# Sparse-attention scores of a decoder layer: native f32 products replaced by three f32r products of high and low parts

## The chip, the cores and the metric

The kernel runs on one core of one Trainium2 chip. The metric is the device time of one execution in microseconds (us). Beside the timed runs there is one profiled execution, and every duration quoted from the trace is of that one.

## What is computed

One decoder layer on 512 tokens of width 1024, in float32: RMSNorm, one combined input projection, two attentions (a sparse one with 8 heads of 64, a dilated one with 12), a gated merge, an output projection, a SwiGLU feed-forward, and a final RMSNorm. The change touches the scores of the sparse attention, for its selected blocks and its window. In the reference, shortened:

```python
def block(i):                                   # 128 queries
    qb = queries * 64 ** -0.5; kb, kwb = keys of the selected blocks, keys of the window
    top, idx = lax.top_k(score, n_top)          # n_top = min(16, 8 blocks): all blocks
    ss = jnp.einsum('bqghd,bgqnld->bghqnl', qb, ks)
    ps, _ = masked_softmax(ss - m * ds, mask_s)   # causal, ALiBi
    o_s = jnp.einsum('bghqk,bgqkd->bqghd', ps, vs)
    sw = jnp.einsum('bqghd,bkgd->bghqk', qb, kwb)
    pw, _ = masked_softmax(sw - m * dw, mask_w)   # the window of 512 covers the sequence
    o_w = jnp.einsum('bghqk,bkgd->bqghd', pw, vwb)
    o = gate_c * o_c + gate_s * o_s + gate_w * o_w
```

With 512 tokens all blocks are selected and the window reaches over the whole sequence, so both branches are full causal attentions with their own keys (two branches b = 0, 1) and the same queries.

## The kernel before

Nearly all dense products are made as three f32r matmuls of high and low parts: `split_product` (L1427 to L1429) adds hi·hi, hi·lo and lo·hi in one PSUM bank. The parts of the weights are made per unit of 256 columns: `split_hi` on ScalarE (L585) casts the raw unit to f32r, `split_lo` on VectorE (L862) subtracts it from the raw values. The small attention products stay native f32.

Every engine walks one list, `SCHEDULE`, and does its own part of each job in that order. From about 223.8 us to 351 us the list interleaves the sparse attention with the projection tiles of the merge gates (units 15 to 21). A tile there is cut in two "parts" of 12 matmuls each. After its second part come "evac" (`gate_of_merge`: VectorE L998 takes it out of PSUM, ScalarE L659 applies tanh) and, for the first tile of a unit, "next_unit" (`split_hi` and `split_lo` of the unit after).

The sparse attention has 20 steps. Step n serves pair j = n // 5 of heads (one in each group, on partitions 0 to 63 and 64 to 127) and the segments of n % 5: (b, i) is branch b, query tile i, whose causal row has 128(i + 1) keys. Each step fills 512 columns of two banks:

```python
NSA_STEPS = [((0, 3),), ((0, 0), (0, 2)), ((0, 1), (1, 1)), ((1, 3),), ((1, 0), (1, 2))]
```

`scores` (L1629) makes them on TensorE, one 64-row matmul per head and segment; the two heads use different halves of the array rows. `reduce` (VectorE, L1176) adds the bias and takes the maximum, `exps` (ScalarE, L676) the exponentials, `scale` (VectorE: L1186, L1197, L1202) the sum's inverse and the gate, `turn` transposes on TensorE (L1642) with a copy by ScalarE (L740), `out` multiplies by v (L1661; for the first step of a pair L1656 too). One round of the list holds two steps: scores n and n + 1; turn n - 2; reduce, exps n; a part; scale n; turn n - 1; reduce, exps n + 1; the second part, its evac and perhaps next_unit; scale n + 1; out. So there are 10 bursts of scores, each of two steps. (In the rounds of n % 5 = 1 out n - 2 comes before turn n - 1.)

In the rounds of n = 8 and n = 12 the end of the list, the same for all engines, is in the code

```python
        parts(1)                                  # tile 44 (46): part, evac, next_unit 19 (20)
        if more:
            jobs.append(("scale", n + 1))
```

and the next round begins with scores 10, 11 (14, 15). Steps 10 and 15 are the first of pairs 2 and 3. Before the first scores stand the dilated attention's last turn and out (L1578, L1597; L719 on ScalarE, L1135 on VectorE) and tile 38, a whole tile of unit 15 (24 matmuls) with `split_hi` and `split_lo` of unit 16.

Of the kernel before, what the change touches and what calls it, by code (L numbers as in the profile page):

```python
# [16 lines left out]
F32 = mybir.dt.float32  # L17
F32R = mybir.dt.float32r
# [5 lines left out]
P = 128  # L24
D = 1024
S = 512
# [55 lines left out]
def schedule():  # L82

    jobs = [("tile", n) for n in range(FIRST_TILE[U_QB + 2] + 1)]
    jobs.append(("cmp_hidden", 0))
    jobs += [("tile", n) for n in range(FIRST_TILE[U_QB + 2] + 1, FIRST_TILE[U_KB])]
    jobs.append(("cmp_spin", 0))
    jobs += [("tile", n) for n in range(FIRST_TILE[U_KB], FIRST_TILE[U_KB + 1])]
    jobs.append(("cmp_kv", 0))
    jobs += [("tile", n) for n in range(FIRST_TILE[U_KB + 1], FIRST_TILE[U_VB])]  # L90
    tile = iter(range(FIRST_TILE[U_VB], len(TILES)))

    def beside(count):
        jobs.extend(("tile", next(tile)) for _ in range(count))

    for m in range(4):
        jobs.append(("dil_scores", m))
        beside(BESIDE_DIL_SCORES[m])
    jobs.append(("dil_merge", 0))
    beside(BESIDE_MERGE)  # L100
    for m in range(4):
        jobs.append(("dil_turn", m))
        if m:
            jobs.append(("dil_out", m - 1))
        beside(BESIDE_DIL_OUT[m])
        jobs.append(("dil_scores", 4 + m))
    beside(BESIDE_CMP[0])
    jobs += [("dil_out", 3), ("dil_merge", 1)]
    beside(BESIDE_CMP[1])
    jobs.append(("cmp_scores", 0))  # L110
    beside(BESIDE_CMP[2])
    jobs.append(("dil_turn", 4))
    beside(BESIDE_CMP[3])
    jobs.append(("cmp_scale", 0))
    beside(BESIDE_CMP[4])
    jobs += [("dil_turn", 5), ("dil_out", 4)]
    beside(BESIDE_CMP[5])
    jobs.append(("cmp_turn", 0))
    jobs += [("dil_turn", 6), ("dil_out", 5)]
    beside(BESIDE_CMP[6])  # L120
    jobs += [("dil_turn", 7), ("dil_out", 6)]
    beside(BESIDE_CMP[7])
    jobs.append(("dil_out", 7))
    beside(BESIDE_CMP[8])
    halves = [(n, 4 * h) for n in tile for h in range(2)]

    def parts(count):
        for _ in range(count):
            n, k = halves.pop(0)
            jobs.append(("part", (n, k)))  # L130
            if k:
                jobs.append(("evac", n))
                if TILES[n][1] == 0:
                    jobs.append(("next_unit", TILES[n][0] + 1))

    jobs += [("scores", 0), ("scores", 1), ("reduce", 0), ("exps", 0), ("reduce", 1), ("exps", 1), ("scale", 0), ("scale", 1)]
    parts(HALVES_NSA[0])
    for n in range(2, NSA_N + 2, 2):
        more = n < NSA_N
        if more:  # L140
            jobs += [("scores", n), ("scores", n + 1)]
        jobs.append(("turn", n - 2))
        if more:
            jobs += [("reduce", n), ("exps", n)]
        parts(1)
        if more:
            jobs.append(("scale", n))
        if n % 5 == 1:
            jobs.append(("out", n - 2))
        jobs.append(("turn", n - 1))  # L150
        if more:
            jobs += [("reduce", n + 1), ("exps", n + 1)]
        parts(1)
        if more:
            jobs.append(("scale", n + 1))
        if n % 5 != 1:
            jobs.append(("out", n - 2))
        jobs.append(("out", n - 1))
    parts(HALVES_NSA[1])
    assert not halves  # L160
    return jobs
# [45 lines left out]
def trunk(nc, x, norm_mix, w_in, pe_k, pe_v, w_ck1, w_ck2, w_cv1, w_cv2, w_up_nsa, w_up_dil,  # L207
          w_out, norm_ffn, w_ffn_in, w_ffn_out, norm_final, out, scratch):
    with ExitStack() as ctx:
# [3 lines left out]
        def at(name, shape, offset, dt=F32):  # L213
# [27 lines left out]
        blk = [at(f"blk_{k}", [PP, 2, CMP], E + 4096 * i) for i, k in enumerate("kv")]  # L241
        dp = at("dil_p", [2, 1920], E)
        dbias = at("dil_bias", [4, 512], E + 15360)
        nbias = [at("nsa_bias0", [2, S], H + 14464), at("nsa_bias1", [2, S], E + 16384)]

        npt = at("nsa_probs_t", [2, 2, 512], Fo)
# [92 lines left out]
        gate_tanh, gate_ready = sem("gate_tanh"), sem("gate_ready")  # L339
        s_ready, s_max, s_exp, p_ready, t_ready, t_evac, o_ready, y_evac = (  # L340
            sem(k) for k in ("s_ready", "s_max", "s_exp", "p_ready", "t_ready", "t_evac", "o_ready", "y_evac"))
        y_hi, y_lo = sem("y_hi"), sem("y_lo")
        ab_ready, m_sum, m_hi, m_lo = (sem(k) for k in ("ab_ready", "m_sum", "m_hi", "m_lo"))
        wo_ready, x2_sum, x2_ss, h_turned, h_hi, h_lo = (
# [234 lines left out]
        def _(act):  # L579
# [85 lines left out]
            def cmp_spin():  # L665
                act.wait_ge(h_spun, 1)
                act.copy(hs[:].rearrange("p m kv c -> p (m kv c)"), ps[3][:, 0:CH]).then_inc(hs_ready, 1)

            def nsa_exps(n):
                segments = nsa_segments(n)  # L670
                for r in range(2):
                    act.wait_ge(s_max, 2 * n + r + 1)
                    for k, (b, i, c, w) in enumerate(segments):
                        v = len(segments) * r + k
                        q = sp[n % 2][:, r, c:c + w]
                        ins = act.activation(q, q, ACT.Exp, scale=-1.0, bias=ust[:, n % 2, 0, v:v + 1],  # L676
                                             accum_out=ust[:, n % 2, 1, v:v + 1])
                ins.then_inc(s_exp, 1)
# [13 lines left out]
            for job, n in SCHEDULE:  # L692
# [4 lines left out]
                elif job == "cmp_spin":  # L697
                    cmp_spin()
                elif job == "dil_scores":
                    g, tiles = DIL_STEPS[n % 4]  # L700
                    for hh in range(2):
                        act.wait_ge(ds_max, 2 * n + hh + 1)
                        for i in tiles:
                            a, b = dil_cuts(g)[i]
                            ins = act.activation(dp[:, hh, a:b], dp[:, hh, a:b], ACT.Exp, scale=-1.0,
                                                 bias=dm[:, g, i, hh:hh + 1], accum_out=dm[:, g, i, 2 + hh:3 + hh])
                    ins.then_inc(ds_exp, 1)
                elif job == "dil_merge":
                    act.wait_ge(de_sub, n + 1)
                    act.activation(de[:], de[:], ACT.Exp).then_inc(de_exp, 1)  # L710
                elif job == "dil_turn":
                    act.wait_ge(dt_ready, 2 * n + 1)
                    if n >= 2:
                        act.wait_ge(do_ready, n - 1)
                    w = 384 if n % 4 == 1 else 512
                    for hh in range(2):
                        if hh:
                            act.wait_ge(dt_ready, 2 * n + 2)
                        act.copy(pt[:, n % 2, hh, 0:w], ps[2 + hh][:, 0:w]).then_inc(dt_evac, 1)  # L719
                elif job == "cmp_scores":  # L720
                    act.wait_ge(cs_sub, 1)
                    act.activation(sc[:], sc[:], ACT.Exp).then_inc(cs_exp, 1)
                elif job == "cmp_turn":
                    for g in range(2):
                        act.wait_ge(ct_ready, g + 1)
                        act.copy(pct[g][:], ps[g][:]).then_inc(pct_ready, 1)
                elif job == "next_unit":
                    split_hi(n)
                elif job == "evac":
                    gate_of_merge(n)  # L730
                elif job == "exps":
                    nsa_exps(n)
                elif job == "turn":
                    if n == 0:
                        act.wait_ge(do_ready, 8)
                    elif n > 1:
                        act.wait_ge(o_ready, n - 1)
                    for r in range(2):
                        act.wait_ge(t_ready, 2 * n + r + 1)
                        act.copy(npt[:, n % 2, r, :], ps[4 + r][:]).then_inc(t_evac, 1)  # L740
                    if n == NSA_N - 1:
                        y_split_hi(0)
                elif job == "out" and n == NSA_N - 1:
                    y_split_hi(1)
# [106 lines left out]
        def _(dve):  # L851
# [364 lines left out]
            for job, n in SCHEDULE:  # L1216
# [19 lines left out]
                    split_lo(n)  # L1236
                elif job == "evac":
                    gate_of_merge(n)
                elif job == "reduce":
                    reduce(n)  # L1240
                elif job == "scale":
# [182 lines left out]
        def _(pe):  # L1424
# [196 lines left out]
            def scores(n):  # L1621
                if n == 0:
                    pe.wait_ge(pct_ready, 2)
                elif n >= 2:
                    pe.wait_ge(s_max, 2 * n - 2)
                segments = nsa_segments(n)
                for b, i, c, w in segments:
                    for r in range(2):
                        ins = pe.matmul(ps[2 * (n % 2) + r][:, c:c + w], qa[rows_of(r), n // 5, P * i:P * i + P],  # L1629
                                        ka[rows_of(r), b, 0:w], start=True, stop=True)  # L1630
                        if (b, i) == segments[-1][0:2]:
                            ins.then_inc(s_ready, 1)

            def turn(n):
                if n:
# [245 lines left out]
```

## Time and profile before

| | |
|---|---|
| median of 3 runs | 805.4 us (805.0 to 805.65) |
| the profiled execution | 805.64 us, its span 803.8 us |
| granted TensorE clock | 0.998 mean over the span |
| TensorE matmul busy | 795.1 us, 99% |
| weight loads busy | 656.6 us, 82% |
| VectorE busy | 404.0 us, 50% |
| ScalarE busy | 287.1 us, 36% |
| scores of the sparse steps, L1629 | 10 bursts, 128 matmul records |

The span is the stretch of the trace from first to last instruction; the time of the execution is 1.8 us more. Matmuls overlap: one record lasts from its start to its modelled end, so the distance between starts, not the record's length, is what a matmul costs in a stream. A native f32 matmul leaves two records, each with its own weight load; an f32r matmul leaves one.

### The profile page before, as it was taken

The numbers are of one execution on the slowest core, as the hardware profiler recorded it, in microseconds if no ns is written. First come the engines' busy times: TensorE is split into PE (matmuls) and PEld (weight loads), VectorE is DVE, ScalarE is ACT, GpSimd is POOL, SyncE is SP. The second block draws the span as 40 slices with busy tenths as digits, with TensorE's granted clock in tenths as the row PEclk, the third lists the DMA queues.
The fourth block names the chain that finished last, engine by engine and source line by source line (L and its number), as shares of the span: only waits on it lengthen the run. The fifth ranks groups of instructions, "written<-read, shape, count | busy, mean of one in ns | idle before, by whom it ended". The sixth has DMA issues, their size and how long they took to land.

```text
span 803.8 us, 11093 instructions
## 1 busy us (share of the span) xinstructions
PE 795.1 (99%) x4354; PEld 656.6 (82%) x4354; DVE 404.0 (50%) x813; ACT 287.1 (36%) x519; POOL 24.8 (3%) x36
## 2 busy tenths in 40 slices
PE   9999999999999999999999999999999999999997
PEld 7778899879877777788888888888888888888885
DVE  5745432645755766647527534443334444323347
ACT  6112155243546565652316312222212223322235
POOL 1301000000000000002200000000000000000000
PEclk9999999999999999999999999999999999999999
DMA  7931345330311111144331243233333222222202
GB/s 236 345 110 53 105 92 144 81 111 4 106 53 53 53 53 41 40 156 130 133 105 53 76 133 87 78 95 104 104 104 102 77 86 102 104 105 104 104 1 105
DMA packets 100215, 79.08 MB, mean 98 GB/s; under 512 B 16928, under 2 KB 94800, under 8 KB 100176
## 3 DMA queue, kind: packets, MB, share of 16 engines
q1 hardware_dynamic: 99936, 78.26, 32.4%
q8 instruction: 26, 0.43, 0.2%
q10 hardware_dynamic: 240, 0.29, 0.1%
q14 instruction: 13, 0.11, 0.0%
HBM read 75.34 MB, written 3.19 MB: 98 GB/s over the span
## 4 chain that ended last, share of the span: by engine, by line
PE 94%; SPq 2%; DMA 2%; ACT 1%; DVE 1%; issue 0%; DVEq 0%; ACTq 0%
PE bank L1427 27%; PE bank L1429 27%; PE bank L1428 27%; PE bank L1642 2%; PE bank L1629 2%; PE bank L1661 2%; PE bank L1556 1%; PE bank L1597 1%; DMA w_raw<-in_w_in_dram 1%; PE bank L1578 1%; PE bank L1519 1%; SPq L469 1%; DMA xs<-in_x_dram 1%; SPq L467 1%; PE bank L1656 1%; ACT w_hi L585 0%
## 5 line engine op out<-in xcount | busy, mean ns | idle before, releaser
L1427 PE MATMUL bank<-h_hi,w_hi 128*128 128x512 f32 (+1 forms) x368 | 140.3, 381 | 0.0
L1428 PE MATMUL bank<-h_lo,w_hi 128*128 128x512 f32 (+1 forms) x368 | 139.8, 380 | 0.0
L1429 PE MATMUL bank<-h_hi,w_lo 128*128 128x512 f32 (+1 forms) x368 | 139.8, 380 | 0.0
L1427 PE MATMUL bank<-n_hi,w_hi 128*128 128x512 f32 x272 | 109.5, 402 | 0.7 <-DVE w_lo L912 0.5
L1429 PE MATMUL bank<-n_hi,w_lo 128*128 128x512 f32 x272 | 106.2, 390 | 0.0
L862 DVE TENSOR_TENSOR w_lo<-w_raw,w_hi 128x2048 fp32r<-128x2048 f32 (+2 forms) x29 | 64.5, 2225 | 82.9 <-ACT w_hi L585 82.9
L1428 PE MATMUL bank<-n_lo,w_hi 128*128 128x512 f32 x272 | 106.0, 390 | 0.0
L1428 PEld LDWEIGHTS bank<-h_lo,w_hi 128*128 128x128 f32 x368 | 69.2, 188 | 13.4 <-issue 0.2
L1427 PEld LDWEIGHTS bank<-h_hi,w_hi 128*128 128x128 f32 x368 | 69.2, 188 | 13.3 <-issue 0.2
L1429 PEld LDWEIGHTS bank<-h_hi,w_lo 128*128 128x128 f32 x368 | 69.2, 188 | 13.0
L782 ACT ACTIVATE tanh_g<-gate_scaled 128x512 f32<-128x512 f32 x22 | 13.9, 632 | 180.9 <-DVE gate_scaled L1311 180.9
L585 ACT CAST w_hi<-w_raw 128x2048 fp32r<-128x2048 f32 (+2 forms) x29 | 53.6, 1848 | 63.2 <-PE bank L1429 45.5
L1311 DVE TENSOR_TENSOR gate_scaled<-bank,rrow 128x512 f32<-128x512 f32 x22 | 15.2, 692 | 108.0 <-PE bank L1429 108.0
L1427 PE MATMUL bank<-w_hi,a_hi 128*128 128x512 f32 (+1 forms) x180 | 69.3, 385 | 0.0
L1429 PE MATMUL bank<-w_hi,a_lo 128*128 128x512 f32 (+1 forms) x180 | 69.2, 384 | 0.0
L1428 PE MATMUL bank<-w_lo,a_hi 128*128 128x512 f32 (+1 forms) x180 | 69.2, 384 | 0.0
L1427 PE MATMUL bank<-w_hi,n_hi 128*128 128x256 f32 (+2 forms) x192 | 62.3, 324 | 0.3 <-ACT va L654 0.3
L1427 PEld LDWEIGHTS bank<-n_hi,w_hi 128*128 128x128 f32 x272 | 51.1, 188 | 13.2 <-issue 3.6
L1428 PE MATMUL bank<-w_lo,n_hi 128*128 128x256 f32 (+2 forms) x192 | 61.4, 320 | 0.0
L1429 PE MATMUL bank<-w_hi,n_lo 128*128 128x256 f32 (+2 forms) x192 | 61.4, 320 | 0.0
L1429 PEld LDWEIGHTS bank<-n_hi,w_lo 128*128 128x128 f32 x272 | 51.1, 188 | 11.0
L1428 PEld LDWEIGHTS bank<-n_lo,w_hi 128*128 128x128 f32 x272 | 51.2, 188 | 9.8 <-issue 0.2
(217 smaller groups left out, 1155.2 us busy)
## 6 DMA issues: line engine op xcount, KB each, us to landing
w_raw<-in_w_ffn_in_dram SPq DMA_DIRECT2D x44, 512.0 KB, 5.0
w_raw<-in_w_in_dram SPq DMA_DIRECT2D x37, 512.0 KB, 4.7
w_raw<-in_w_ffn_out_dram SPq DMA_DIRECT2D x22, 512.0 KB, 3.6
w_raw<-in_w_out_dram SPq DMA_DIRECT2D x8, 512.0 KB, 4.1
w_raw<-in_w_in_dram SPq DMA_DIRECT2D x12, 256.0 KB, 4.5
xs<-in_x_dram SPq DMA_DIRECT2D x4, 512.0 KB, 7.0
wck_k<-in_w_ck_dram SPq DMA_DIRECT2D x1, 2048.0 KB, 11.9
wck_v<-in_w_cv_dram SPq DMA_DIRECT2D x1, 2048.0 KB, 17.5
```

The lines of the kernel that those rows point to most:

```text
L467: sp_.dma_start(wck[kv][:], w[0].rearrange("(a p) n -> p a n", p=P)).then_inc(wck_in[kv], 16)
L469: sp_.dma_start(w2k[:, :, r, :], w_ck2[0].rearrange("(m p) d -> p m d", p=P)).then_inc(w2_in, 16)
L585: act.copy(whi[u % 2][:, 0:n], raw[u % 2][:, 0:n]).then_inc(hi_done, 1)
L782: act.activation(tg[:, s, :], gs[:, s, :], ACT.Tanh, scale=0.5).then_inc(gu_tanh, 1)
L862: dve.tensor_tensor(wlo[u % 2][:, 0:n], raw[u % 2][:, 0:n], whi[u % 2][:, 0:n].bitcast(F32), ALU.subtract).then_inc(lo_done, 1)
L1311: dve.tensor_tensor(gs[:, s, :], ps[2 * s][:], rrow[:], ALU.mult).then_inc(g_scaled, 1)
L1427: pe.matmul(dst, w[0], x_[0], start=start, stop=False)
L1428: pe.matmul(dst, w[0], x_[1], start=False, stop=False)
L1429: return pe.matmul(dst, w[1], x_[0], start=False, stop=stop)
L1629: ins = pe.matmul(ps[2 * (n % 2) + r][:, c:c + w], qa[rows_of(r), n // 5, P * i:P * i + P], ka[rows_of(r), b, 0:w], start=True, stop=True)
L1642: ins = pe.transpose(ps[4 + r][:, c:c + P], sp[n % 2][:, r, c:c + P], ident[:])
L1661: ins = pe.matmul(o[rows_of(r), P * i:P * i + P], va[:, k, 128 * b + HD * r:128 * b + HD * r + HD], npt[:, n % 2, r, c + P * k:c + P * k + ...
```

## The change

K and q are split into an f32r high part (ScalarE) and a low part (VectorE): k once before the scores, in a job "parts_of_k"; q once for each pair of heads in "parts_of_q", into two buffers in turn. In the list, parts_of_k and parts_of_q(0) stand before tile 38, parts_of_q(1) after scale 1, parts_of_q(2) after scale 9 and parts_of_q(3) after scale 13. `scores` makes three f32r products hi·hi, hi·lo, lo·hi for each head and segment, on the same 64-row halves; the two segments of 256 columns of steps with n % 5 = 2, which share a query tile, become one matmul of 512 columns.

```diff
-    jobs += [("scores", 0), ("scores", 1), ("reduce", 0), ("exps", 0), ("reduce", 1), ("exps", 1), ("scale", 0), ("scale", 1)]
+    jobs += [("parts_of_k", 0), ("parts_of_q", 0)]
+    beside(BESIDE_CMP[8])
+    halves = [(n, 4 * h) for n in tile for h in range(2)]
+    jobs += [("scores", 0), ("scores", 1), ("reduce", 0), ("exps", 0), ("reduce", 1), ("exps", 1), ("scale", 0), ("scale", 1),
+             ("parts_of_q", 1)]
...
         if more:
             jobs.append(("scale", n + 1))
+            if n in (8, 12):
+                jobs.append(("parts_of_q", n // 4))
...
+        khl = at("k_parts", [2, 2, S], E + 8192, F32R)
+        qhl = [at("q_parts0", [2, S], Dd + 32768, F32R), at("q_parts1", [2, S], E + 20480, F32R)]
...
+            def k_parts_hi():
+                act.wait_ge(tile_evac_dve, evac_count(LAST_TILE[U_KA]))
+                act.wait_ge(dt_ready, 16)
+                act.copy(khl[:, 0], ka[:]).then_inc(k_hi, 1)
+
+            def q_parts_hi(j):
+                if j == 0:
+                    act.wait_ge(do_ready, 8)
+                if j >= 2:
+                    act.wait_ge(s_ready, 10 * j - 10)
+                act.copy(qhl[j % 2][:, 0], qa[:, j]).then_inc(q_hi, 1)
...
+                elif job == "parts_of_k":
+                    dve.wait_ge(k_hi, 1)
+                    dve.tensor_tensor(khl[:, 1], ka[:], khl[:, 0].bitcast(F32), ALU.subtract).then_inc(k_lo, 1)
+                elif job == "parts_of_q":
+                    dve.wait_ge(q_hi, n + 1)
+                    dve.tensor_tensor(qhl[n % 2][:, 1], qa[:, n], qhl[n % 2][:, 0].bitcast(F32), ALU.subtract).then_inc(q_lo, 1)
...
+                j = n // 5
+                pe.wait_ge(k_lo, 1)
+                pe.wait_ge(q_lo, j + 1)
                 segments = nsa_segments(n)
-                for b, i, c, w in segments:
-                    for r in range(2):
-                        ins = pe.matmul(ps[2 * (n % 2) + r][:, c:c + w], qa[rows_of(r), n // 5, P * i:P * i + P],
-                                        ka[rows_of(r), b, 0:w], start=True, stop=True)
-                        if (b, i) == segments[-1][0:2]:
-                            ins.then_inc(s_ready, 1)
+                blocks = [(slice(b, b + 1), i, c, w) for b, i, c, w in segments]
+                if n % 5 == 2:
+                    blocks = [(slice(0, 2), 1, 0, 256)]
+                for both, i, c, w in blocks:
+                    wide = w * (both.stop - both.start)
+                    for k, (x_, y_) in enumerate(((0, 0), (0, 1), (1, 0))):
+                        for r in range(2):
+                            ins = pe.matmul(ps[2 * (n % 2) + r][:, c:c + wide], qhl[j % 2][rows_of(r), x_, P * i:P * i + P],
+                                            khl[rows_of(r), y_, both, 0:w], start=(k == 0), stop=(k == 2))
+                            if k == 2 and i == blocks[-1][1]:
+                                ins.then_inc(s_ready, 1)
```

## Rows read from the trace of the kernel before

**Rows 1.** The page's busy line and its chain by engine.
```profile
PE 795.1 (99%) x4354; PEld 656.6 (82%) x4354; DVE 404.0 (50%) x813; ACT 287.1 (36%) x519; POOL 24.8 (3%) x36
...
PE 94%; SPq 2%; DMA 2%; ACT 1%; DVE 1%; issue 0%; DVEq 0%; ACTq 0%
```

**Rows 2.** The chain in order of time: start, us, what; two of ten bursts of scores.
```profile
283.82 1.93 PE bank L1629 x12
...
307.12 1.93 PE bank L1629 x12
```

**Rows 3.** The same chain: other native f32 and narrow matmuls, and a transposing stretch.
```profile
171.19 1.09 PE bank L1556 x16
...
195.45 3.52 PE bank L1609 x32
...
451.83 0.86 PE bank L1669 x2
```

**Rows 4.** TensorE in order of time: start us, us, op; f32r streams of 256 and 512 columns.
```profile
128.37 0.28 PE L1428 MATMUL bank<-w_lo,n_hi 128*128 128x256 f32 x1
...
134.84 0.28 PE L1428 MATMUL bank<-w_lo,n_hi 128*128 128x256 f32 x1
...
279.27 0.39 PE L1428 MATMUL bank<-n_lo,w_hi 128*128 128x512 f32 x1
...
281.54 0.39 PE L1429 MATMUL bank<-n_hi,w_lo 128*128 128x512 f32 x1
281.86 1.97 PE L1661 MATMUL bank<-nsa_probs_t,va 128*64 128x128 f32 x32
```

**Rows 5.** VectorE and ScalarE by form: casts and subtractions of the split kind, mean ns.
```profile
L903 DVE TENSOR_TENSOR w_lo<-w_raw,w_hi 128x512 fp32r<-128x512 f32 x4 | 2.7, 687 | 0.3 <-ACT w_hi L596 0.3
...
L912 DVE TENSOR_TENSOR w_lo<-w_raw,w_hi 128x1024 fp32r<-128x1024 f32 x2 | 2.4, 1216 | 0.0
...
L601 ACT CAST w_hi<-w_raw 128x1024 fp32r<-128x1024 f32 x2 | 2.1, 1046 | 0.0
...
L596 ACT CAST w_hi<-w_raw 128x512 fp32r<-128x512 f32 x3 | 1.8, 611 | 0.0
```

**Rows 6.** All engines in order of time, ahead of the first scores.
```profile
215.87 1.07 ACT L719 COPY probs_t<-bank 128x512 f32<-128x512 f32 x2 [0.75 <-PE bank L1578]
...
218.22 1.09 DVE L1135 TENSOR_TENSOR yb<-bank,yb 128x512 f32<-128x512 f32 x1 [2.33 <-PE bank L1597]
...
223.76 2.00 PE L1629 MATMUL bank<-ka,qa 64*128 64x512 f32 x12
```

**Rows 7.** VectorE in order of time after step 1, and the chain's third burst of scores.
```profile
229.71 1.15 DVE L1202 TENSOR_SCALAR probs<-probs,ust 128x128 f32<-128x128 f32 x4
...
232.09 0.69 DVE L998 SCALAR_TENSOR_TENSOR gm<-bank,rrow 128x512 f32<-128x512 f32 x1
...
248.98 1.93 PE bank L1629 x12
```

**Rows 8.** VectorE and ScalarE in order of time, end of the round of steps 8 and 9.
```profile
281.96 0.69 DVE L998 SCALAR_TENSOR_TENSOR gm<-bank,rrow 128x512 f32<-128x512 f32 x1 [1.26 <-PE bank L1429]
...
283.23 1.88 ACT L585 CAST w_hi<-w_raw 128x2048 fp32r<-128x2048 f32 x1
...
285.14 2.29 DVE L862 TENSOR_TENSOR w_lo<-w_raw,w_hi 128x2048 fp32r<-128x2048 f32 x1 [2.48 <-ACT w_hi L585]
287.35 0.17 DVE L1186 RECIPROCAL ust<-ust 128x4 f32<-128x4 f32 x1
...
288.81 0.69 DVE L1176 CUSTOM_DVE_ANT_0 probs<-bank,nsa_bias 128x512 f32<-128x512 f32 x1
```

**Rows 9.** The same for the round of steps 12 and 13.
```profile
304.40 0.69 DVE L998 SCALAR_TENSOR_TENSOR gm<-bank,rrow 128x512 f32<-128x512 f32 x1
...
307.59 2.29 DVE L862 TENSOR_TENSOR w_lo<-w_raw,w_hi 128x2048 fp32r<-128x2048 f32 x1 [2.50 <-ACT w_hi L585]
309.80 0.16 DVE L1186 RECIPROCAL ust<-ust 128x2 f32<-128x2 f32 x1
...
310.98 0.29 DVE L1176 CUSTOM_DVE_ANT_0 probs<-bank,nsa_bias 128x128 f32<-128x128 f32 x1
```

**Rows 10.** TensorE in order of time: its first work, and its last.
```profile
1.06 3.35 PE L1438 MATMUL bank<-ones 128*128 128x128 f32 x14 [1.06 <-DVE ones L892]
...
4.63 1.34 PE L1451 MATMUL bank<-ident,xs 128*128 128x128 f32 x8
...
797.63 0.28 PE L1429 MATMUL bank<-w_hi,a_lo 128*128 128x256 f32 x1
```

**Rows 11.** Windows: us, busy of PE, PEld, DVE, ACT, POOL, granted clock, DMA, GB/s.
```profile
799.00:801.00 2.00, 0.00 (x0) 0.00 (x0) 1.35 (x7) 1.00 (x2) 0.00 (x0) 0.87 0.58 238
801.00:803.80 2.80, 0.00 (x0) 0.00 (x0) 0.00 (x0) 0.02 (x1) 0.00 (x0) 0.50 0.50 187
```

**Rows 12.** Waits: idle of VectorE before scale, by what ended it: total us, times, longest.
```profile
DVE ust L1186 <- ACT probs L676: 15.4, 15, 1.5
```

More of the change, by code:

```diff
@@ L123, in schedule @@
     jobs.append(("dil_out", 7))
-    beside(BESIDE_CMP[8])
-    halves = [(n, 4 * h) for n in tile for h in range(2)]
+    halves = []
     def parts(count):
@@ L341, in trunk @@
             sem(k) for k in ("s_ready", "s_max", "s_exp", "p_ready", "t_ready", "t_evac", "o_ready", "y_evac"))
+        k_hi, k_lo, q_hi, q_lo = (sem(k) for k in ("k_hi", "k_lo", "q_hi", "q_lo"))
         y_hi, y_lo = sem("y_hi"), sem("y_lo")
@@ L732, in _ @@
                     nsa_exps(n)
+                elif job == "parts_of_k":
+                    k_parts_hi()
+                elif job == "parts_of_q":
+                    q_parts_hi(n)
                 elif job == "turn":
@@ L1238, in _ @@
                     gate_of_merge(n)
+                elif job == "parts_of_k":
+                    dve.wait_ge(k_hi, 1)
+                    dve.tensor_tensor(khl[:, 1], ka[:], khl[:, 0].bitcast(F32), ALU.subtract).then_inc(k_lo, 1)
+                elif job == "parts_of_q":
+                    dve.wait_ge(q_hi, n + 1)
+                    dve.tensor_tensor(qhl[n % 2][:, 1], qa[:, n], qhl[n % 2][:, 0].bitcast(F32), ALU.subtract).then_inc(q_lo, 1)
                 elif job == "reduce":
```

## The prediction

> **What bounds the kernel now.** I read the busy line and the chain that ended last first: TensorE is busy 99% of the span and holds 94% of the chain [rows 1]. Going through TensorE's records in order of time I found no idle stretch over 0.5 us after its first instruction. So the time is TensorE's stream: a matmul made shorter comes straight off the end, and a wait of TensorE goes straight onto it. VectorE (50%) and ScalarE (36%) have room on average, but an average says nothing of where they stand when TensorE asks for a particular result. That needs the second view, VectorE and ScalarE in order of time around each new wait.
>
> **What the scores cost now.** A burst of two steps takes 1.93 us, and there are ten, 19.3 us in all [rows 2]. Its content is 1,024 columns for each of two heads. The native f32 matmul of 512 columns over the whole array takes 0.86 us for two records, 0.42 ns for each of 4 passes of a column [rows 3]; 4 × 1,024 × 0.4167 = 1.71 us would be one head's share. The burst costs that plus 0.22 us: the two heads run side by side, and 0.2 us goes for changing into and out of this shape of array.
>
> **What they cost as f32r.** A stream of f32r matmuls over the whole array steps by 0.227 us at 512 columns (10 steps in 2.27 us) and by 0.120 us at 256 (54 steps in 6.47 us) [rows 4]: one pass at 0.4167 ns a column plus 13 ns. At 384 columns that is 0.173 us. At 128 columns it would be 0.066 us, but a matmul does not come faster than its weights: 32 narrow matmuls, each with 128 columns of weights, take 3.52 us, 0.110 us each [rows 3]. The trace has no f32r matmul below 256 columns and none on 64 rows. I take 0.110 us for 128 columns, next to the 256-column row; the upper end is the four passes of native f32, 4 × 128 × 0.4167 = 0.213 us. For two heads I take the price of one, because the native pairs show it: 16 records of 128 columns with their 16 weight loads take 1.09 us [rows 3], 0.068 us each, less than the 0.110 us of one load over the whole array, so loads of different halves run side by side as well.
>
> Steps by n % 5, three products each: 0, 2 and 3 are one block of 512, 3 × 0.227 = 0.68 us; 1 and 4 are 128 and 384, 3 × (0.110 + 0.173) = 0.85 us. Five steps make 3.74 us, twenty 14.95 us, and ten changes of shape 2.0 to 2.2 us more. Against 19.3 us **the products save 2.3 us**, at best 3.2 (without the 13 ns), at worst nothing: 8 blocks of 128 columns × 3 × 0.103 us = 2.5 us takes it back.
>
> Whether the loads stay hidden on 64 rows, where each head's next product uses the same rows as the one in flight, no row shows. For the full array they do: at 0.227 us for 512 columns (0.213 us of columns) [rows 4] no load of 0.110 us fits between. The Trainium skill ("TensorE: Matmul & The Clock Gate", Part 3, "What overlaps and what doesn't") says that a weight load overlaps a running matmul only when it goes to another row group. By that rule the scores would cost more than now (rival D); the full-array rows disagree with it.
>
> **The splits.** ScalarE gets one cast of 1,024 columns (1.05 us) and four of 512 (0.61 us); VectorE one subtraction of 1.22 us and four of 0.69 us [rows 5]. In sum 3.5 us and 4.0 us, on engines with room. The places matter.
>
> k and q(0): ScalarE is free of the dilated copies at 216.9 us; k's high part is there at 218.0, q's at 218.8 (it waits for the last dilated out, at 218.2). VectorE adds up yb from 218.22 for 1 us [rows 6], then both low parts until about 221.2. The scores ask at 223.76 [rows 6]. Covered by tile 38, 2.6 us to spare; without that cover TensorE would wait these 3 us. The split of unit 16, queued behind, ends near 223.4 instead of 221.4 and is needed only with tile 40, which follows tile 39 at about 231.5. q(1) follows scale 1, whose last operation starts at 229.71, and the bias of pair 1, and is first used at step 5, in the burst that starts at 248.98 [rows 7]: hidden. It moves the evacuation of tile 39, now at 232.09 [rows 7], by 0.7 us, and its bank is next written by out 0, after the scores at 236.9. Both cost nothing.
>
> q(2) is different. Scores 10 stand first in the round after steps 8 and 9, and now wait for q_lo 3, which VectorE reaches only after scale 9. Follow VectorE in the present trace [rows 8]: it empties tile 44 at 281.96, waits for ScalarE's tanh and for the cast of unit 19 (283.23, 1.88 us), subtracts (285.14, 2.29 us), begins scale 9 at 287.35 and is free at 288.81, where reduce 10 starts now. There the subtraction of q goes, 0.69 us, to 289.5. Its high part was cast at 285.1, in time. TensorE asks at 283.82 [rows 2]. So it waits until about 289.55: **5.7 us**. Before, nothing tied scores 10 to scale 9; the split of unit 19 and scale 9 ran under scores, a turn and a part. Queued on TensorE behind scores 10 are scores 11, turn 8, part 45 and all that follows, so none of them can fill the hole. The start of this chain is the end of tile 44 on TensorE, so the products saved earlier move both ends alike and don't shorten it.
>
> q(3) has the same form: tile 46 leaves at 304.40, unit 20 is subtracted from 307.59, scale 13 starts at 309.80 and ends at 310.98 [rows 9]; with 0.69 us the low part is there at 311.7. Scores 15 ask after scores 14, at 307.12 + 0.85 = 308.0 [rows 2]. **3.7 us.** What comes late next, reduce 10 and reduce 15, is asked for by turn 10 and turn 15 a round later, and VectorE's waits for exponentials there are at most 1.5 us [rows 12]; no third wait follows.
>
> **The clock.** TensorE's last matmul ends at 797.9, and the granted clock is 0.87 over 799 to 801 and 0.50 after [rows 10, 11]: with 1 before and 0.5 behind, it falls at 800.5, 2.6 us after the work stopped. Both new holes are longer. Coming back is seen at the start: 14 records from 1.06 us take 3.35 us, 0.239 us each where the full clock gives 0.107, and the next 8 take 1.34 us, 0.167 each [rows 10]; so the first 4 us or so ran at 1.2 GHz rather than 2.4. Four microseconds at half speed do the work of two: 2.0 us lost after the first hole. The second exceeds the 2.6 us by only 1.1, so I count 1.5 us. **3.5 us**, between 0 and, with both stretches half as long again, 6.
>
> **The sum.** Against the profiled execution, 805.64 us (span 803.8 and 1.8 around it): −2.3 + 5.7 + 3.7 + 3.5 = +10.6, 816.2 us. The median of the runs lies 0.2 lower: **816.0 us**.
>
> **The rivals.**
> A. The clock stays up in the holes. The only fall in the trace has no work behind it, so this can't be excluded. 816.0 − 3.5 = 812.5 us. Chance 0.12.
> B. f32r matmuls of 128 columns run at the four-pass price: +2.5 us, 818.5 us. No row at 128 speaks against it; 256 and 280 columns run at one pass. Chance 0.18.
> C. The two heads' f32r matmuls don't run side by side. The products then cost twice 14.95 us: +15, 831 us. The native pairs speak against it. Chance 0.06.
> D. Loads to the rows of the running matmul are not hidden, so each of the 84 pair products (21 a pair of heads) shows its load of 0.110 us before its columns. A step of 512 becomes 3 × (0.110 + 0.227) = 1.01 us, one of 128 and 384 3 × (0.110 + 0.066 + 0.110 + 0.173) = 1.38 us; together 23.2 instead of 14.95 us, +8.3: 824 us. The full-array stream speaks against it. Chance 0.04. (This is the rule of the Trainium skill's page "TensorE: Matmul & The Clock Gate", named above.)
> E. The other side: the waits don't arise. The place is VectorE's turn before scores 10 and 15: if q_lo 3 came by 283.8 and q_lo 4 by 308.0, only the saving is left, 803.1 us. It decides between forecast and gain from the point where the two holes with their clock are under 2.3 us together, against 9.4 us of holes worked out. It needs VectorE to reach parts_of_q before the split of units 19 and 20, and the order of the list is against that. Chance 0.06.
>
> The forecast has the remaining 0.54.
>
> **How the numbers follow.** The low end is rival A with the products at their best: 805.4 + 9.4 − 3.2 = 811.6. The high end is B with the clock at 4.5 us, 819.5, widened to 820.5 for clock stretches of uneven length. 811.5 to 820.5 holds the forecast, A and B, 0.84, less the tails of each. C, D and E are outside. 0.2% (1.6 us) is about what a measurement of this kernel can tell from none. Faster is E, 0.06 less a little: 0.05; within 0.2% 0.02; slower 0.93.
>
> **What would show it.** In the changed kernel's trace: two idle stretches of TensorE ahead of L1629's successor, 5.7 and 3.7 us, ended by VectorE's low part of q, and none at pairs 0 and 1; the VectorE order w_lo, scale, q's low part before them; a granted clock of 0.5 for some 4 us after the first; bursts of scores of about 1.5 to 1.75 us elsewhere, with starts of the two heads' matmuls within a few ns. A burst above 1.93 us would speak for B, C or D, and the steps' widths tell which. The prediction is wrong if VectorE subtracts q before unit 19, or if the bursts are longer than now.

## The result, and the profile after

The changed kernel takes 817.75 us (median of 4 runs, 816.57 to 818.22), the kernel before 805.52 us in the same comparison: ratio 1.0147, 95% interval 1.0134 to 1.0159. It is 12 us slower; the forecast was 816.0 us, in a range of 811.5 to 820.5. The profiled execution took 818.22 us with a span of 816.4.

The page's first lines of the changed kernel, which answer to [rows 1]:

```profile
PE 798.5 (98%) x4394; PEld 664.0 (81%) x4394; DVE 407.7 (50%) x818; ACT 291.2 (36%) x524; POOL 24.8 (3%) x36
...
PEclk9999999999999988999999999999999999999999
...
PE 92%; DVE 2%; SPq 2%; ACT 2%; DMA 1%; issue 0%; ACTq 0%; DVEq 0%
```

The totals hardly tell anything: VectorE and ScalarE are busy 4 us more each. But two slices of the clock line have an 8 where all were 9, and the chain goes 2% over VectorE and 2% over ScalarE, which before had 1% each. The chain in order of time says where (start, us, what):

```profile
223.93 1.76 PE bank L1667 x18
...
236.83 1.59 PE bank L1667 x12
...
248.57 1.75 PE bank L1667 x18
...
281.00 0.70 DVE gm L1022
281.75 0.51 issue
282.26 1.89 ACT w_hi L593
284.17 2.29 DVE w_lo L886
286.79 1.14 DVE probs L1226 x4
287.93 0.61 DVE q_parts L1268
288.67 3.25 PE bank L1667 x18
```

The first three lines are bursts of scores: 1.75 us where a step has a block of 128 columns, 1.59 us where none has, against 1.93 us before [rows 2]. The last seven are the forecast's chain to the letter: tile 44 out of PSUM, tanh (in "issue", its record is on ScalarE), the cast of unit 19, its subtraction, scale 9, q's low part, scores 10. TensorE in order of time shows the same two places as idle time with its releaser:

```profile
288.67 3.25 PE L1667 MATMUL bank<-k_parts,q_parts 64*128 64x512 f32 x18 [5.82 <-DVE q_parts L1268]
...
318.40 1.65 PE L1667 MATMUL bank<-k_parts,q_parts 64*128 64x512 f32 x6 [3.63 <-DVE q_parts L1268]
```

The burst after the first hole takes 3.25 us instead of 1.75. The windows say why (us, busy of PE, PEld, DVE, ACT, POOL, granted clock, DMA share, GB/s):

```profile
282.86:286.60 3.74, 0.00 (x0) 0.00 (x0) 2.39 (x3) 1.80 (x2) 0.00 (x0) 1.00 0.00 0
286.60:288.67 2.07, 0.00 (x0) 0.03 (x1) 1.89 (x6) 0.00 (x0) 0.00 (x0) 0.50 0.46 109
288.67:293.42 4.75, 4.75 (x26) 4.12 (x27) 0.00 (x0) 0.36 (x1) 0.00 (x0) 0.50 0.51 177
...
314.76:317.30 2.54, 0.01 (x2) 0.00 (x0) 2.47 (x5) 0.00 (x0) 0.00 (x0) 1.00 0.00 0
317.30:318.40 1.10, 0.00 (x0) 0.03 (x1) 0.95 (x2) 0.00 (x0) 0.00 (x0) 0.51 0.13 34
318.40:324.14 5.74, 5.74 (x20) 4.54 (x21) 1.47 (x8) 2.51 (x8) 0.00 (x0) 0.50 0.53 130
```

A "hole" is such an idle stretch of TensorE. After 3.7 us of standing still in the first hole and 2.5 us in the second the granted clock goes to 0.5 (1.2 GHz), and it stays there 4.75 and 5.74 us into the work that follows. Work at half speed takes twice its time, so half of that is lost: 2.4 + 2.9 = 5.2 us. The balance of the spans: 803.8 − 2.1 (8 bursts × 0.18, 2 × 0.34) + 5.8 + 3.6 + 5.2 = 816.3, measured 816.4.

### The profile page after: what moved, and what is told of

It is laid out like the page before. It is cut to its first block, busy times and chain, and to the rows that moved or that the text cites. A ratio compares the mean times of both kernels' runs of the same rounds, so it can differ in the third digit from the quotient of the medians.

```text
span 816.4 us, 11204 instructions
## 1 busy us (share of the span) xinstructions
PE 798.5 (98%) x4394; PEld 664.0 (81%) x4394; DVE 407.7 (50%) x818; ACT 291.2 (36%) x524; POOL 24.8 (3%) x36
## 4 chain that ended last, share of the span: by engine, by line
PE 92%; DVE 2%; SPq 2%; ACT 2%; DMA 1%; issue 0%; ACTq 0%; DVEq 0%
PE bank L1457 27%; PE bank L1458 26%; PE bank L1459 26%; PE bank L1680 3%; PE bank L1667 2%; PE bank L1699 2%; PE bank L1586 1%; SPq L477 1%; PE bank L1627 1%; ACT w_hi L593 1%; PE bank L1608 1%; DMA w_raw<-in_w_in_dram 1%; PE bank L1549 1%; DVE w_lo L886 1%; SPq L475 1%; PE bank L1481 0%
```

## The experiments

Ratios are to the kernel before, run beside each on the same chip, with the 95% interval in brackets.

**1. Both late splits one round earlier.** The cause in the forecast is where q(2) and q(3) stand, so only that is changed.

```diff
-            if n in (8, 12):
-                jobs.append(("parts_of_q", n // 4))
+            if n in (6, 10):
+                jobs.append(("parts_of_q", (n + 2) // 4))
```

> The changed kernel with parts_of_q(2) and parts_of_q(3) each one round of the list earlier, after scale 7 and scale 11, in rounds that split no unit. If the loss is the low part of q coming late on VectorE, with the clock that falls in the two holes, both holes and both falls of the clock go and the saving of the bursts is left, (1.93 - 1.72) x 10 = 2.1 us: 803.4 us, about 0.26% faster than before. Rival, the added casts and subtractions cost time wherever they stand: 805.5 us or above. Rival, the waits on q_lo hold TensorE for another reason than their place: two holes ahead of scores stay, 815 us or more.

803.3 us, ratio 0.9974 (0.9964 to 0.9983); span 801.1. VectorE of this kernel in order of time:

```profile
273.30 1.14 DVE L1226 TENSOR_SCALAR probs<-probs,ust 128x256 f32<-128x256 f32 x4
274.36 0.69 DVE L1268 TENSOR_TENSOR q_parts<-qa,q_parts 128x512 fp32r<-128x512 f32 x1
```

and the chain at scores 10:

```profile
282.19 1.74 PE bank L1667 x11
```

The lines are scale 7 and, right behind it, the subtraction that gives q(2)'s low part. It is there at 275 us, 7 us ahead of the scores that want it. Both holes are gone, the mean granted clock is 0.999 again, and what is left is the saving. This is faster than the kernel before and the changed kernel.

**2. Same round, but ahead of the split of the weights.**

```diff
             jobs += [("reduce", n + 1), ("exps", n + 1)]
+            if n in (8, 12):
+                jobs.append(("parts_of_q", n // 4))
         parts(1)
```

> parts_of_q(2) and (3) stay in the rounds of steps 8 and 12, but stand after exps 9 (13), ahead of the second part, its evac and the split of units 19 and 20. If what makes them late is what they stood behind on VectorE, the low part of q is there at about the time at which TensorE asks, no hole above 0.5 us is left: 803.4 to 804.2 us; the evacuation of tiles 44 and 46 comes up to 1.4 us later and is hidden. Rival, the round itself is too full for them: part of the holes stays, 808 us or more.

805.8 us, ratio 1.0004 (0.9995 to 1.0013): 12 us better than the changed kernel, but 2.5 us short of experiment 1. The holes ahead of the scores are gone; two others have come, ahead of turns 9 and 13 (TensorE in order of time):

```profile
289.29 1.09 PE L1680 MATMUL bank<-ident,probs 128*128 128x128 f32 x8 [0.71 <-DVE probs L1226]
...
313.56 1.06 PE L1680 MATMUL bank<-ident,probs 128*128 128x128 f32 x8 [1.29 <-DVE probs L1226]
```

VectorE now evacuates tile 44 later by q's wait and subtraction, so the cast, the subtraction of unit 19 and scale 9 are all later, and turn 9 wants scale 9; the same goes for tile 46, scale 13 and turn 13. I had called that hidden, with evacuations up to 1.4 us later. Against the scores of the next round they moved by 1.5 us (tile 44) and 3.1 us (tile 46), and the cover in the kernel before was 0.7 us for turn 9 (VectorE free of scale 9 at 288.81, the turn at 289.55) and 1.8 us for turn 13 (310.98, 312.83). 0.71 + 1.29 = 2.0 us of the 2.5.

**3. The holes kept, but filled.** Matmuls whose result is overwritten, ahead of the wait (they are extra work).

```diff
+                for f in range({10: 20, 15: 13}.get(n, 0)):
+                    pe.matmul(ps[2 * (n % 2)][:], nhi[:, 0, 0:P], nhi[:, f % 8, :], start=True, stop=True)
                 pe.wait_ge(q_lo, j + 1)
```

> The changed kernel with both holes kept and filled: ahead of the wait for q_lo, scores 10 issue 20 and scores 15 issue 13 full-array f32r matmuls of 512 columns (0.227 us each, 4.5 and 2.9 us) into the bank that the first product then overwrites. The waits end when they did. If the low clock is a cost of its own that comes from TensorE standing still, the granted clock stays at 1 and 4.75/2 + 5.74/2 = 5.2 us come back: 812.5 us. Rival, the clock falls anyway or its fall costs nothing beside the wait: 817.7 us. Rival, the filling delays the scores: above 818 us.

813.72 us, ratio 1.0104 (1.0088 to 1.0119), span 810.8. TensorE stands still for only 0.98 and 0.37 us, the waits end as late as ever (288.01 us), and the clock holds:

```profile
280.00:287.00 7.00, 7.00 (x54) 5.40 (x52) 4.02 (x8) 3.74 (x7) 0.00 (x0) 1.00 0.01 3
287.00:288.00 1.00, 0.03 (x1) 0.00 (x0) 0.96 (x3) 0.00 (x0) 0.00 (x0) 1.00 0.79 157
288.00:295.00 7.00, 6.99 (x49) 5.99 (x50) 2.98 (x11) 3.43 (x8) 0.00 (x0) 1.00 0.37 128
```

The span is 5.6 us shorter than the changed kernel's, of which 0.6 lies ahead of the first scores (they start at 223.28 us here and at 223.85 there). That agrees with the 5.2 expected, but the profiled execution was the fastest of the four here and the slowest of four for the changed kernel: the medians differ by 4.0 us, and the difference of the two ratios, 0.0043, is 3.5 us with an uncertainty of 1.5 to 2. So the low clock is a cost of its own, beside the wait; its size in the timed runs is less sure than that it is there.

**4. The splits alone.** The order of experiment 1, with all casts, subtractions and waits, but `scores` makes the native products from q and k as before (the parts are computed and not used).

> The splits alone: casts and subtractions of k and q, their buffers and the waits of scores for them, parts_of_q(2) and (3) a round earlier, but the products are native f32 as before and read k and q themselves. If the splits are hidden, 805.5 us, no difference to before; if ScalarE or VectorE time counts, up to 7.5 us more (813 us). Against the kernel with f32r products in the same order this gives the saving of the products by itself: 2.1 us expected.

805.57 us, ratio 0.9999 (0.999 to 1.0008). Where they are early enough, the splits cost nothing that these runs can tell, which is to about 0.7 us. Against experiment 1 the f32r products are worth 0.0025, 2.0 us, with an uncertainty of up to 1 us.

**5. The waits alone.** The order of the change, native products.

> The waits alone: splits and waits where the change put them, products native f32. Both holes and both falls of the clock stay, the saving goes. Holes 5.8 + 3.6, clock 2.4 + 2.9: 805.5 + 14.7 = 820.2 us, less up to 0.1 where scores 14 end inside the second hole: 820 us. Rival, the loss comes from the f32r products themselves: 806 us or less.

821.98 us, ratio 1.0184 (1.0163 to 1.0204), which is 14.8 us. The holes are 5.82 and 3.62 us. So the loss needs no f32r product at all. The windows of both holes, from the fall of the clock on:

```profile
289.96:290.96 1.00, 0.00 (x1) 0.03 (x1) 0.85 (x2) 0.00 (x0) 0.00 (x0) 0.50 0.93 252
290.96:296.79 5.83, 5.83 (x21) 3.76 (x22) 0.11 (x1) 0.70 (x2) 0.00 (x0) 0.50 0.38 134
...
320.68:321.79 1.11, 0.00 (x0) 0.03 (x1) 0.96 (x2) 0.00 (x0) 0.00 (x0) 0.50 0.10 30
321.79:327.51 5.72, 5.72 (x17) 3.83 (x18) 1.47 (x8) 2.07 (x5) 0.00 (x0) 0.50 0.53 132
```

After a first hole of the same 5.82 us as in the changed kernel the clock is low for 5.83 us of the work and not 4.75: here it fell 4.8 us after the hole began, there 3.7. So 2.9 + 2.9 us are lost to the clock. The span is 16.6 us longer than before: 9.4 of holes, 5.8 of clock, and 1.3 from the part ahead of the first scores (225.08 us against 223.76), which the change does not explain.

**6. Only q(2) earlier.**

```diff
-            if n in (8, 12):
-                jobs.append(("parts_of_q", n // 4))
+            if n in (6, 12):
+                jobs.append(("parts_of_q", (n + 2) // 4))
```

> The changed kernel with only parts_of_q(2) a round earlier; parts_of_q(3) stays behind unit 20 and scale 13. One hole of 3.6 us before scores 15 and one stretch of low clock, of which about 2.9 us are lost: 803.4 + 6.5 = 809.9 us. If the clock's fall needed the first hole too: 807.0 us.

810.97 us, ratio 1.0056 (1.0037 to 1.0074), 4.5 us. The one hole left drops the clock by itself:

```profile
306.90:308.90 2.00, 0.00 (x1) 0.00 (x0) 1.92 (x1) 0.57 (x2) 0.00 (x0) 1.00 0.00 0
308.90:311.20 2.30, 0.00 (x0) 0.02 (x1) 2.09 (x6) 0.00 (x0) 0.00 (x0) 0.50 0.05 15
311.20:315.70 4.50, 4.49 (x17) 3.59 (x18) 0.91 (x7) 1.27 (x3) 0.00 (x0) 0.50 0.65 167
```

Hole 4.3 us, 0.7 more than in the changed kernel. There VectorE stood ready when TensorE ended tile 46 (it had waited 0.56 us); here it came from reduce 13 without a pause, and ScalarE from exps 13 to the tanh. Probably the first hole had let both catch up; that is not tested. Clock 4.5 / 2 = 2.2 us.

**7. One head's three products issued before the other's**, in the order of experiment 1.

```diff
-                    for k, (x_, y_) in enumerate(((0, 0), (0, 1), (1, 0))):
-                        for r in range(2):
+                    for r in range(2):
+                        for k, (x_, y_) in enumerate(((0, 0), (0, 1), (1, 0))):
```

> As the kernel with both parts_of_q a round earlier, but the three products of one head are issued before those of the other (r outside k). If the saving rests on the two heads' matmuls running side by side, a burst of scores costs up to twice 1.5 us: about 3.0 to 3.2 us, +13 to +15 us, 816 to 818 us. If TensorE puts them side by side by itself, or takes them one by one anyway, no difference: 803.4 us.

803.38 us, ratio 0.9966 (0.9951 to 0.9982), and the first burst of the chain is

```profile
223.24 1.77 PE bank L1667 x18
```

where experiment 1 has 1.76. The first of the two expectations missed: three matmuls of one half of the rows in front of those of the other half do not keep them apart. This left open whether side by side is worth anything, so they were forced apart:

**8. The two heads of a step kept apart by a wait.**

```diff
+                for r in range(2):
+                    if r:
+                        pe.wait_ge(s_ready, 2 * n + 1)
```

with the blocks and the three products inside r.

> As the kernel with both parts_of_q a round earlier, with the products of the second head of a step held back by a wait until the first head's last product has ended. It sizes rival C of the prediction, the two heads not side by side. Products 15 us more, and for each of 20 steps the end of a matmul that is otherwise overlapped, about 0.2 us, 4 us: 822 us. If the side-by-side running of the two heads gave nothing: 807 us, the ends alone.

819.18 us, ratio 1.0164 (1.0147 to 1.0181). The same burst, TensorE in order of time, and the forms of its matmuls (busy us, mean ns):

```profile
223.76 3.40 PE L1669 MATMUL bank<-k_parts,q_parts 64*128 64x512 f32 x18
```

```profile
L1669 PE MATMUL bank<-k_parts,q_parts 64*128 64x512 f32 x72 | 21.3, 425 | 0.7
L1669 PE MATMUL bank<-k_parts,q_parts 64*128 64x384 f32 x48 | 11.7, 350 | 0.0
L1669 PE MATMUL bank<-k_parts,q_parts 64*128 64x128 f32 x48 | 8.6, 287 | 0.5
```

The next tile starts 3.33 us after the start of this burst (at 227.09), against 1.76: +1.57 us, and +1.42 for the two bursts without a block of 128 columns, 15.6 us in ten. Against experiment 1 the medians differ by 15.9 us, the ratios by 15.3. In experiment 1 the three forms are busy for about half of that:

```profile
L1667 PE MATMUL bank<-k_parts,q_parts 64*128 64x512 f32 x72 | 10.6, 408 | 0.0
L1667 PE MATMUL bank<-k_parts,q_parts 64*128 64x384 f32 x48 | 5.9, 350 | 0.0
L1667 PE MATMUL bank<-k_parts,q_parts 64*128 64x128 f32 x48 | 4.0, 271 | 0.0
```

So within a step the two heads run side by side in experiment 1 and one after the other here. But that the sum comes out at rival C's 15 us is in part luck, for the wait holds back only the second head of its own step. The same burst in three windows, cut where a waiting head starts (us, busy of PE and PEld with their counts, granted clock, DMA share, GB/s, for this line alone):

```profile
223.76:224.78 1.02, 0.96 (x3) 0.48 (x3) 1.00 0.38 36
224.78:226.03 1.25, 1.20 (x9) 0.88 (x9) 1.00 0.92 291
226.03:227.09 1.06, 1.05 (x6) 0.81 (x6) 1.00 1.09 386
```

The middle one holds nine matmuls, three of 512 columns and three each of 128 and 384: the second head of the first step and the first head of the second step run side by side, which one after the other would be 0.68 + 0.85 = 1.53 us. Against this stands the handover: across the first wait the starts of two matmuls lie 0.45 us apart where the same product otherwise follows after 0.24, across the second 0.39 us against 0.17. That is 0.2 us for each of 20 steps, the 4 us expected. The expected 822 us are not reached because of the overlap of neighbouring steps, not because the wait is free.

**9. Half the filling of experiment 3**, 10 and 7 matmuls, so that TensorE stands still 3.24 and 1.73 us.

> As the kernel with the filled holes, with half the filling: 10 matmuls before scores 10, 7 before scores 15, so that TensorE stands still for about 3.4 and 1.9 us. Holes of 0.7 to 1.3 us did not drop the clock in the runs so far, holes of 3.6 us and more did, 2.0 to 3.7 us after they began. If the length decides, the first hole drops it and the second does not: 2.4 to 2.9 us of low clock, 815.5 us. If the filling work itself keeps it up: 812.8 us. If any late wait drops it: 818 us.

814.66 us, ratio 1.0113 (1.0093 to 1.0134), span 813.0. The second hole leaves the clock alone. The first drops it, but only after it has ended:

```profile
285.42:288.66 3.24, 0.00 (x1) 0.00 (x0) 3.12 (x8) 0.00 (x0) 0.00 (x0) 1.00 0.26 48
288.66:289.28 0.62, 0.62 (x6) 0.53 (x8) 0.00 (x0) 0.00 (x0) 0.00 (x0) 1.00 1.06 377
289.28:292.69 3.41, 3.41 (x23) 2.88 (x20) 0.00 (x0) 0.15 (x1) 0.00 (x0) 0.50 0.58 198
```

3.41 us at half speed, 1.7 lost, where 2.4 to 2.9 had been expected.

## Why the prediction was right

**The number and the parts.** The measured 817.75 us lies 1.7 us above the forecast and only 0.8 below rival B's 818.5, so the number alone would rather speak for B. The parts decide.

**The saving.** Forecast 2.3 us, measured 2.1 in the bursts and 2.0 in the ratios of experiments 1 and 4. The price of 0.110 us for 128 columns, taken from weight loads of another shape [rows 3], fits: 0.68 + 3 × (0.110 + 0.173) + 0.2 = 1.73 against bursts of 1.75. Rival B would have made them 2.04. Rival D, loads not hidden on the rows in use, would have made the 1.59 us bursts 2 × 1.01 + 0.2 = 2.2. Rival D's rule, that a weight load overlaps a running matmul only on another row group, is from the Trainium skill ("TensorE: Matmul & The Clock Gate", Part 3, "What overlaps and what doesn't"). The bursts of 1.59 us disagree with it. Rival C fell with the same bursts; its price of 15 us is worked out and not measured by itself, since experiment 8 keeps only the two heads of a step apart and adds waits.

**The splits.** Hidden, as worked out: experiment 4. In the changed kernel VectorE's parts of k and q(0), by form 1.227 and 0.688 us, end at 221.1, forecast 221.2.

**The first hole.** Forecast 5.7 us, measured 5.8. **The second**: 3.7 and 3.6. Experiment 1 removes both by moving the two jobs one round earlier in the list, experiment 5 has both without the products. That no third wait follows was right as well.

**The clock.** The mechanism was right, the size was off: "Four microseconds at half speed do the work of two: 2.0 us lost after the first hole ... I count 1.5 us" for the second, 3.5 in all; measured 2.4 + 2.9 = 5.2 us. The stretches at half speed lasted 4.75 and 5.74 us into the work, and the second hole, which I had marked down for being short, cost more than the first. The step that failed is the one that read the recovery off the kernel's start and assumed a shorter hole gives a shorter stretch. The windows show something else. Counted from the fall of the clock to its rise, five stretches lasted 6.8 us each: 2.07 us in the hole and 4.75 in the work, 1.10 and 5.74 in the changed kernel; 1.00 and 5.83, 1.11 and 5.72 in experiment 5; 2.30 and 4.50 in experiment 6. Experiment 9's lasted 3.41 us, all in the work. So what the work loses is half of what is left of the stretch when the hole ends, and in the shorter hole less of it had passed. Rival A (clock stays up, 812.5 us) fell with the windows, and experiment 3 (813.7) is about what it would have looked like. The 1.7 us here are nearly all of what the forecast lacked.

**The other side.** Rival E was what the change could have been: its 803.1 us is experiment 1's 803.3.

What stays open: the lengths of the low stretches are read, not explained, and so is the place of the fall, which came 2.0 to 4.8 us after the hole began, at different places for the same hole (3.7 and 4.8 us). And the profiled executions differ before the change comes into play: the first burst of scores starts at 223.26 us in experiment 1, at 223.93 in the changed kernel, at 224.13 in experiment 2, about 225.1 in experiment 5. So spans can be compared to 1 or 2 us only, and the 0.5 us between experiments 1 and 2 that lie in no hole are not settled.

## What to carry to other kernels

A new input of an instruction on the bound engine is late by everything that stands ahead of its producer in that producer's queue, however idle the producer is on average: here a 0.7 us subtraction behind a weight split and a scale cost 5.8 us, and the same work one round earlier cost nothing. Ask for each new wait when its producer reaches it in the trace of before, and move the producer past nothing that another wait depends on (experiment 2). Where a dense kernel gets a hole of several microseconds, add the clock: half of the low stretch that reaches into the work after it, here 5.2 us on top of 9.4 us of holes. The shorter of two holes can cost more of it, as here.

## What the runs showed of the hardware that was not expected

- Matmuls on the two 64-row halves run side by side even when three of one half are issued ahead of the other's: burst 1.77 us against 1.76 interleaved, and 3.33 where the second head of each step waits for the first.
- The clock's fall can come after the hole has ended: 0.62 us into the work after a hole of 3.24 us. Holes of 0.37 to 1.73 us left it at 1 (5 of 5), holes of 3.2 us and more dropped it (6 of 6).
- The time at half speed does not follow the hole's length: 4.75 and 5.83 us into the work after holes of 5.82, 5.74 and 5.72 after 3.6, 4.5 after 4.3, 3.41 after 3.24. From fall to rise it was 6.8 us in five cases of six and 3.41 in one.
- A wait of TensorE for the end of its own preceding matmul costs 0.2 us: 0.45 us between starts in place of 0.24, and 0.39 in place of 0.17 (experiment 8). The chain shows only 0.04 us of it as "issue", because it counts the rest as the end of the matmul waited for.
